# Inverses of the delta rule's chunks: the two lower levels multiply blocks of 64, the top level one block

## The reference, cut to what matters

```python
a_mat = jnp.where(strict, beta[..., :, None] * kk * decay, 0.0)
t_mat = lax.linalg.triangular_solve(eye + a_mat, eye, left_side=True, lower=True)
w_c, u_c = t_mat @ (beta * k * exp(gc)), t_mat @ (beta * v)
# step over chunks:
v_new = u - w @ state
o = q_dec @ state + qk @ v_new
state = state * exp(g_last) + k_dec.T @ v_new
```

## Time and profile before

| | us |
|---|---|
| median of 3 runs | 2405.39 (2403.96 to 2406.69) |
| profiled execution, its own time | 2402.13 |
| its span | 2400.3 |
| PE busy | 2317.5 (97%) |
| DVE busy | 1581.2 (66%) |
| ACT busy | 1106.5 (46%) |
| POOL busy | 1090.5 (45%) |
| mean granted TensorE clock | 0.988 |

### The profile page before, as it was taken

The page is one execution under the profiler, slowest core; times in us unless marked ns, Lnnn a source line. Parts: engine busy times, 40 slices in busy tenths (PEclk is TensorE's granted clock), DMA queues, the critical chain, the costliest instruction groups (busy, mean ns, idle before and its releaser), DMA issues.

```text
span 2400.3 us, 31290 instructions
## 1 busy us (share of the span) xinstructions
PE 2317.5 (97%) x11427; PEld 1843.5 (77%) x11427; DVE 1581.2 (66%) x2124; ACT 1106.5 (46%) x1960; POOL 1090.5 (45%) x690
## 2 busy tenths in 40 slices
PE   8999989998998999999999999999999999999997
PEld 6778877776786888878788777676778788888885
DVE  7854267664577655496746968868878765545754
ACT  5652235554344555543545546556533332225552
POOL 2212266562334766655787411111114665556763
PEclk9999999999998999999999999999999999999998
DMA  4113242215323544574543321111123343338553
GB/s 160 44 49 106 92 141 84 83 49 171 114 71 139 177 150 147 183 266 150 174 141 120 106 71 45 45 36 45 43 78 117 125 148 106 105 131 297 183 162 139
DMA packets 148261, 287.51 MB, mean 120 GB/s; under 512 B 27107, under 2 KB 39651, under 8 KB 148108
## 3 DMA queue, kind: packets, MB, share of 16 engines
q1 hardware_dynamic: 148108, 285.51, 35.9%
HBM read 206.99 MB, written 78.46 MB: 119 GB/s over the span
## 4 chain that ended last, share of the span: by engine, by line
PE 82%; DVE 9%; issue 3%; ACT 3%; DMA 2%; POOL 1%; SPq 0%; POOLq 0%; DVEq 0%; ACTq 0%
PE bank L604 11%; PE bank L608 11%; PE bank L606 11%; PE bank L805 11%; PE bank L803 11%; PE bank L801 10%; PE bank L674 5%; PE bank L892 2%; PE bank L866 2%; PE bank L879 2%; ACT t L925 1%; DVE t L1327 1%; DMA t<-in_wf 1%; PE bank L770 1%; PE bank L788 1%
## 5 line engine op out<-in xcount | busy, mean ns | idle before, releaser
L1975 POOL TENSOR_TENSOR t<-t,t 128x512 fp32r<-128x512 f32 (+1 forms) x494 | 810.5, 1651 | 1069.5 <-ACT t L925 1046.9
L925 ACT ACTIVATE t<-t 128x512 fp32r<-128x512 f32 (+1 forms) x688 | 448.8, 676 | 690.7 <-PE bank L805 280.0
L604 PE MATMUL bank<-t,t 128*128 128x512 f32 x1360 | 551.4, 405 | 11.3 <-ACT t L925 11.1
L608 PE MATMUL bank<-t,t 128*128 128x512 f32 x1360 | 533.6, 392 | 4.6 <-DVE t L1327 3.4
L606 PE MATMUL bank<-t,t 128*128 128x512 f32 x1360 | 532.4, 391 | 0.0
L801 PE MATMUL bank<-t,t 128*128 128x512 f32 x1316 | 516.3, 392 | 9.5 <-ACT t L925 6.8
L805 PE MATMUL bank<-t,t 128*128 128x512 f32 x1316 | 515.7, 392 | 7.0 <-DVE t L1327 6.5
L803 PE MATMUL bank<-t,t 128*128 128x512 f32 x1316 | 515.2, 391 | 4.0 <-POOL t L1975 4.0
L604 PEld LDWEIGHTS bank<-t,t 128*128 128x128 f32 x1360 | 256.9, 189 | 76.4 <-issue 22.8
L608 PEld LDWEIGHTS bank<-t,t 128*128 128x128 f32 x1360 | 256.6, 189 | 62.6 <-DVE t L1327 5.1
L606 PEld LDWEIGHTS bank<-t,t 128*128 128x128 f32 x1360 | 257.0, 189 | 54.4 <-issue 4.5
(11 more groups left out here) (238 smaller groups left out, 2580.3 us busy)
## 6 DMA issues: line engine op xcount, KB each, us to landing
t<-in_w SPq DMA_DIRECT2D x87, 512.0 KB, 3.6
hid_scr<-t SPq DMA_DIRECT2D x112, 256.0 KB, 2.3
t<-hid_scr SPq DMA_DIRECT2D x112, 256.0 KB, 2.7
t<-in_wf SPq DMA_DIRECT2D x80, 256.0 KB, 3.4
t<-in_wf SPq DMA_DIRECT2D x36, 512.0 KB, 4.5
g_scr<-t SPq DMA_DIRECT2D x36, 512.0 KB, 2.9
t<-g_scr SPq DMA_DIRECT2D x72, 256.0 KB, 3.7
t<-in_wo SPq DMA_DIRECT2D x24, 512.0 KB, 3.7
```

What stands on the lines that cost most here:

```text
L604: e.matmul(ps[:, :], hi[:, w, :], XH[:, x, hs], start=k == 0, stop=False)
L608: last = e.matmul(ps[:, :], hi[:, w, :], XL[:, x, hs], start=False, stop=k == j.nk - 1)
L925: return e.activation(out, in_, ACT.Copy, **kw)
L1975: return e.tensor_tensor(out, x, high.bitcast(F32), ALU.subtract)
```

## The change

For the lower two levels `la` and `lb` multiply only the two diagonal blocks of 64: for each head two products 64x64x64, one with rows 0 to 63 into partitions 0 to 63, one with rows 64 to 127 into partitions 64 to 127, and both write columns 64 j to 64 j + 63, so a bank's first 256 columns are used. `lp` masks 128 elements a partition instead of 256 and keeps `P` in the first 64 columns of a head; `lt` becomes two operations, one for each half of the partitions. At the top level `la` and `lb` are four products 64x64x64, in one quarter of the array, into the place of the one new block; `lp` is a copy of that block without a mask, `lt` a subtraction in it, both on 64 partitions. The masks of the lower levels shrink to 32 columns, and the top level has none. Waits, banks and semaphores stay.

```diff
+HALVES = slice(0, 64), slice(64, 128)
+def v64(ps):
+    return ps[:, 0:256].rearrange("p (j c) -> p j c", j=4)
+def top_block(d):
+    return HALVES[1 - d], HALVES[d]
...
+    def block_heads(ps, a, b):
+        for j in range(4):
+            for h in HALVES:
+                last = e.matmul(ps[h, 64 * j:64 * j + 64], a[h, j, h], b(j, h), start=True, stop=True)
+        return last
+    def top_heads(ps, d, a, b, inner):
+        rows, c = top_block(d)
+        for j in range(4):
+            last = e.matmul(ps[rows, 128 * j + c.start:128 * j + c.stop], a[inner, j, rows], b[inner, j, c], start=True, stop=True)
+        return last
...
 def la(d, i, l):
-        heads(prep_bank("la", d, i, l), lambda j: buf(d, i, "AT")[:, j, :], lambda j: buf(d, i, "T")[:, j, :]).then_inc(*tick("la", d, i, l))
+        ps = prep_bank("la", d, i, l)
+        if l == TOP:
+            top_heads(ps, d, buf(d, i, "AT"), buf(d, i, "T"), top_block(d)[1]).then_inc(*tick("la", d, i, l))
+        else:
+            block_heads(ps, buf(d, i, "AT"), lambda j, h: buf(d, i, "T")[h, j, h]).then_inc(*tick("la", d, i, l))
...
 def lp(d, i, l):
-        tt(cols(M.unit(d, i, "P")[:, :, :], b, d), cols(v4(K.prep_bank("la", d, i, l)), b, d), msk, ALU.mult).then_inc(*tick("lp", d, i, l))
+        if l == TOP:
+            rows, c = top_block(d)
+            e.tensor_copy(M.unit(d, i, "P")[rows, :, c], v4(K.prep_bank("la", d, i, l))[rows, :, c]).then_inc(*tick("lp", d, i, l))
+        else:
+            msk = C(f"lv{d}_{b}").rearrange("p (k b) -> p k b", b=b).unsqueeze(1).broadcast_to([128, 4, 32 // b, b])
+            tt(cols(M.unit(d, i, "P")[:, :, 0:64], b, d), cols(v64(K.prep_bank("la", d, i, l)), b, d), msk, ALU.mult).then_inc(*tick("lp", d, i, l))
...
 def lt(d, i, l):
-        tt(T, T, cols(v4(K.prep_bank("lb", d, i, l)), LEVELS[l], d), ALU.subtract).then_inc(*tick("lt", d, i, l))
+        if l == TOP:
+            last = tt(T[rows, :, c], T[rows, :, c], v4(ps)[rows, :, c], ALU.subtract)
+        else:
+            for h in HALVES:
+                own = cols(T[h, :, h], LEVELS[l], d)
+                last = tt(own, own, cols(v64(ps)[h], LEVELS[l], d), ALU.subtract)
```

More of the change, by code:

```diff
@@ L723, in lb @@
             q.wait_ge(done("ltt", d, i, l - 1))
-        heads(prep_bank("lb", d, i, l), lambda j: buf(d, i, "TT")[:, j, :], lambda j: buf(d, i, "P")[:, j, :]).then_inc(*tick("lb", d, i, l))
+        ps = prep_bank("lb", d, i, l)
+        if l == TOP:
+            top_heads(ps, d, buf(d, i, "TT"), buf(d, i, "P"), top_block(d)[0]).then_inc(*tick("lb", d, i, l))
+        else:
+            block_heads(ps, buf(d, i, "TT"), lambda j, h: buf(d, i, "P")[h, j, 0:64]).then_inc(*tick("lb", d, i, l))
     def lx(d, i, l):
@@ L1446, in lp @@
         b = LEVELS[l]
-        msk = C(f"lv{d}_{b}").rearrange("p (k b) -> p k b", b=b).unsqueeze(1).broadcast_to([128, 4, 64 // b, b])
         q.wait_ge(done("la", d, i, l))
@@ L1450, in lp @@
             q.wait_ge(done("sc", d, i))
-        tt(cols(M.unit(d, i, "P")[:, :, :], b, d), cols(v4(K.prep_bank("la", d, i, l)), b, d), msk, ALU.mult).then_inc(*tick("lp", d, i, l))
+        if l == TOP:
[4 more added lines that the diff above has]
+            tt(cols(M.unit(d, i, "P")[:, :, 0:64], b, d), cols(v64(K.prep_bank("la", d, i, l)), b, d), msk, ALU.mult).then_inc(*tick("lp", d, i, l))
     def lt(d, i, l):
-        T = cols(M.unit(d, i, "T")[:, :, :], LEVELS[l], d)
         q.wait_ge(done("lb", d, i, l))
@@ L1459, in lt @@
             q.wait_ge(done("tex", d, i))
-        tt(T, T, cols(v4(K.prep_bank("lb", d, i, l)), LEVELS[l], d), ALU.subtract).then_inc(*tick("lt", d, i, l))
+        T, ps = M.unit(d, i, "T"), K.prep_bank("lb", d, i, l)
+        if l == TOP:
+            rows, c = top_block(d)
+            last = tt(T[rows, :, c], T[rows, :, c], v4(ps)[rows, :, c], ALU.subtract)
+        else:
+            for h in HALVES:
+                own = cols(T[h, :, h], LEVELS[l], d)
+                last = tt(own, own, cols(v64(ps)[h], LEVELS[l], d), ALU.subtract)
+        last.then_inc(*tick("lt", d, i, l))
     def cr(d, i):
@@ L3202, in constants @@
     c["neg16"] = np.broadcast_to(np.where(a > b, 0, NEG).astype(f), (128, 256)).copy()
-    q = np.arange(64)[None, :]
-    for b in LEVELS:
-        same = s // (2 * b) == q // b
+    q = np.arange(32)[None, :]
+    for b in LEVELS[:TOP]:
+        same = s % 64 // (2 * b) == q // b
         c[f"lv0_{b}"] = (same & ((s // b) % 2 == 1)).astype(f)
```

## The result

The changed kernel takes 2384.5 us in the median (2381.78 to 2385.57, four runs) against 2404.69 (2403.96 to 2406.69): ratio 0.9913, interval 0.9896 to 0.993. A second set on another chip gave 2379.72 against 2403.01, ratio 0.9904 (0.9889 to 0.9919). The kernel is 20 to 23 us faster. The forecast was 2389, 16 us.

The account below looks back on a forecast made before the run. TensorE, busy 97% of the span, was taken as the bound. 41.1 us of passes less 15.6 of switches left 25.4; two thirds, 17, minus 3 for clock plus 2 of tail gave 16: 2389 us, range 2378 to 2410.

Parts of the forecast that it names:

- The pass and the switch: PE, la and lb: 0.058 us passes save 41.1 us; 91 more shape switches at 0.172 cost 15.6; net 25.4 less.
- DVE: lp and lt: narrow lp 283 ns, 4.3 us less; lower lt 4.8 us more; +0.5 us in all, hidden in idle.
- What arrives: Inverses' stage: two thirds of the 25.4 us, 17, reach the end; minus 3 for clock, plus 2 at the tail: 16.
- The term of the clock: Stage: more idle on PE brings more time at 1.2 instead of 2.4 GHz, costing 3 us.
- The order: All engines: changed planner costs rewrite the order, unreadable beforehand; PE idle a few us more or less, +-4 us.
- the first: Rival, lower la and lb: two quarters don't overlap or small records have a floor; 4.5 us slower, time 2411; 13%.
- The floor of 0.062 us a record: Part of the 13% rival on lower la and lb: each record takes at least 0.062 us, 8.6 us slower.
- The chain binds: Rival, middle of the stage: lp, lt, ltt and signals set the pace; only 3 to 6 us arrive, 2400.5; 17%.
- the clock: Rival: thinner array work lowers granted rate from 0.97 to 0.90 over 300 us, 21 us more; 2405 or above; 6%.
- the sign that was named: Clock below 0.93 over 314 to 600 us would show that the clock rival is the true one.

Follow-up runs that it names:

- e1: New products, masks and subtractions, but planner costs of la, lb, lp, lt held at old values, so the order of the kernel before: 2389.27 us, ratio 0.9947.
- e6: Changed kernel in its own order, with every la and lb issuing its products twice into the same place: 2403.68 us.
- e4: Kernel before, in its order, with blocks of 64 only at the two lower levels; top level left old: 2391.62 us, ratio 0.996.
- e3: Changed kernel, but each lower-level group runs one quarter's four products and then the other's, instead of in turn: 2392.9 us, ratio 0.9958 to the kernel before.
- e5: Kernel before, in its order, with one block of 64 only at the top level; lower levels left old: 2396.56 us, ratio 0.9969.
- e2: Old products, masks and subtractions of the kernel before, planned with the changed kernel's costs, so only the order is new: 2393.6 us, ratio 0.9961.
- s20: Changed kernel planned with measured costs, ready PE steps of the array's present shape preferred by 0.2 of rank: 2371.65 us, ratio 0.9872 to the kernel before.
- s00: Changed kernel planned with measured costs: 470 ns per la and lb, 170 ns per shape change, aqk and apv recosted: 2375.1 us, ratio 0.9887 to the kernel before.
- s26: As s20, with the preference for the array's present shape at 0.26 of rank instead of 0.2: 2379.63 us, ratio 0.9904 to the kernel before.

## Why the prediction was right, point by point

1. *The pass and the switch.* 0.058 us and 0.10 + 0.05 or 0.10 + 0.10 are what the timeline shows to the second figure. The 195 changes of shape that were counted are what e1's stage has, in the old order (197 in the changed kernel's own), and the work fell by 28.4 us where 25.4 was the sum. The 3 us more are not settled. Two things may work that way, neither measured by itself: a switch next to a wait costs less than between two full groups (some 17 switches' worth would do), and neighbours in different quarters overlap, which the sum left out.
2. *DVE.* 284 and 287 ns for 283, +0.8 us for +0.5, hidden.
3. *What arrives.* "Two thirds" was too much for the whole change. e1 says 13.0 of 28.2 (46%), e6 24.0 of 43.7 (55%). Smaller steps arrived in greater part: 64% in e4, about 12 of 14.2 us in e3, and in e5 more than the work itself. The term of the clock was put at 3 us; in e1's slow execution it is 10.1, in the changed kernel's two 5.3 and 7.8. Here the step was mis-sized: idle and the clock together hold back half of a cut of 28 us. Which waits the idle is made of was not parted.
4. *The order.* "+-4 us" was the term that failed: e2 shows 8.7 us for it alone. Without it the forecast of 16 would have met 13; with it the change is 20 to 23. That the time fell so well inside 2379 to 2398 is in part luck: the arriving part was taken too large and the order at zero, and the two errors cancel.
5. *The rivals.* Quarters of one bank overlap (partners 7 ns apart, 1.15 us for 32 records), so the first is out. The Trainium skill's page "TensorEngine Tiling (Array Packing)", section "Gotcha 1: PSUM Pressure", says that different row tiles cannot access one bank at the same time. Here two row tiles write different partitions of one bank, and they do it at full pace, so the measurement decides. The floor of 0.062 us a record is out too, with two records every 0.058 (the 8.6 us that this floor was to cost come to about 9.4 by its own terms). *The chain binds* and *the clock* each hold in part. Idle went from 28.0 to 37.9 us, as the prediction's 30 to 38 said. The clock passed the sign that was named, below 0.93 over 314 to 600: here it is 0.92, in the kernel before 0.96. But the price of 21 us for it did not come, as half-rate time in which PE was busy rose by 10.6 us only. These stretches, of before and after:

```profile
314.00:600.00 286.00, 258.21 (x1871) 207.94 (x1872) 184.09 (x376) 149.93 (x396) 165.88 (x108) 0.96 0.35 109
...
314.00:600.00 286.00, 249.44 (x2361) 187.22 (x2362) 196.65 (x419) 157.82 (x413) 172.37 (x114) 0.92 0.37 116
```

And the whole stage of the kernel after, beside the same row of before under e2:

```profile
285.50:588.20 302.70, 264.78 (x2584) 200.24 (x2584) 194.70 (x425) 156.87 (x412) 167.03 (x110) 0.93 0.34 106
```

Its PE busy is 23 us lower, its DVE busy 4 us higher (a stretch of another length), and 0.97 has become 0.93.

## What to carry to other kernels

Price a product of blocks as passes plus what a change of array shape costs on both sides (here 0.058 us a pass and about 0.17 us a change), and let products of different quarters alternate; at some 0.9 us of full products per group, as here, an isolated group wins little (0.08 us by the prediction's sum) and neighbours win most. Where a planner orders the engines, a change of any cost is a new order: measure the old work in the new order and the new work in the old one before you credit either, and put the switch into the planner (s20: 8 us more). Of 28 us of work taken from a full engine about half came back here, as idle and as half rate.

## What the runs showed of the hardware

- Two products in different quarters of the array, writing different partitions of the same columns of one bank, run side by side at full pace (two records every 58 ns). A later one starts ahead of three older ones of a busy quarter, beside the fifth of the eight (e3). The Trainium skill's page "TensorE: Matmul & The Clock Gate", section "The mechanism", has MATMULs strictly in program order and only loads pulled ahead; the starts in e3 and of L740 beside L747 in s20 are out of that order, and the measurement decides.
- 64 partitions cost DVE as much as 128 at the same width: a subtraction of 256 elements takes 417 and 415 ns.
- A change of the array's shape costs 0.09 to 0.10 us of emptying, and the first load behind it is bare: 0.05 us for 64 columns, 0.10 for 128. By s00 and s20 it is 0.16 us a change in all.
- Half rate (1.2 of 2.4 GHz): the stage had 14 to 48 us of it in all, idle part included: 20.5 before, 48.3 in e1 with 10 us of idle more, 39.7 after, and 14.9 in e6, where 43.7 us of repeated products fill the gaps. The sum of idle doesn't set it: e4 and s26 idle for 35.4 and 39.1 us and have 17.1 and 20.5 us of half rate. Where the waits lie seems to matter; no run parts this.
